# Gate projections ahead of split branch projections, and expert rows picked by a 0/1 matrix, in a hybrid encoder step

## The reference

```python
z = x @ w_in                       # q, k, v | xr | gr | gl: 768 + 1024 + 1024 + 2048 columns
attn = sink_attention(rope(q), rope(k), v)          # 8 heads, chunks of 64, a window of two chunks and the meta keys
rnn = scan(a, u)(conv(xr)) * gelu(gr)               # RG-LRU, gates from two block-diagonal products
g = sigmoid(gl + b_gate)                            # 1024 for attention, 1024 for the recurrence
mix = (g_attn * (attn @ w_branch_attn) + g_rnn * (rnn @ w_branch_rnn)) @ w_out
x = layer_norm(ALPHA * x + mix)
# hierarchical experts: best group of 4, best two of its 4 experts
for e in range(16):
    h = silu(x @ w_gate[e]) * (x @ w_up[e])         # 1024 -> 512
    y = y + combine[:, e:e+1] * (h @ w_down[e])     # 512 -> 1024
x = layer_norm(ALPHA * x + y)
```

## Time and profile before

| | us |
|---|---|
| median of 3 runs (636.44 to 639.0) | 638.3 |
| the profiled execution | 637.03 |
| its span | 635.2 |
| TensorE matmuls busy (84% of the span) | 536.4 |
| VectorE busy | 230.0 |
| ScalarE busy | 133.5 |
| GpSimd busy | 68.5 |

### The profile page before, as it was taken

How to read it: one execution, slowest core, us unless ns; L and a number is a source line. 1 busy time by engine, 2 the same in 40 slices (tenths; PEclk the granted TensorE clock), 3 DMA queues, 4 the chain that set the end, 5 groups by cost and what they waited for, 6 DMA issues and landing times.

```text
span 635.2 us, 9071 instructions
## 1 busy us (share of the span) xinstructions
PE 536.4 (84%) x3552; PEld 393.7 (62%) x3553; DVE 230.0 (36%) x488; ACT 133.5 (21%) x245; POOL 68.5 (11%) x87
## 2 busy tenths in 40 slices
PE   4789989999999999999973699899787898687840
PEld 1789956887889798878663465555443455354410
DVE  2925985777332223113346021211111111111177
ACT  3344287852512122100020000000000000000010
POOL 4160730000000000010000710100000000000210
PEclk9999989877999999999975799999879799989895
DMA  8237791402156879790075389999999999999642
GB/s 220 98 97 219 191 297 44 134 1 68 33 194 203 299 247 313 268 358 10 33 308 205 100 318 385 381 387 376 391 397 401 414 412 410 397 423 426 252 124 83
DMA packets 55213, 157.49 MB, mean 248 GB/s; under 512 B 3558, under 2 KB 36034, under 8 KB 51076
## 3 DMA queue, kind: packets, MB, share of 16 engines
q1 hardware_dynamic: 46464, 135.11, 57.0%
q0 software_dynamic: 4896, 13.92, 7.6%
q10 hardware_dynamic: 3812, 7.88, 3.5%
HBM read 145.10 MB, written 11.78 MB: 247 GB/s over the span
## 4 chain that ended last, share of the span: by engine, by line
PE 66%; DMA 15%; DVE 7%; issue 4%; ACT 3%; SPq 3%; DVEq 0%; POOL 0%; POOLq 0%; ACTq 0%
PE bank L1031 20%; DMA expert_slots<-in_w_up 10%; PE bank L842 8%; PE bank L992 7%; PE bank L829 6%; PE bank L830 6%; PE bank L831 6%; SPq L590 3%; PE bank L917 3%; PE bank L1024 2%; DMA z_rows<-work 2%; PE bank L811 1%; PE bank L897 1%; PE bank L812 1%; PE bank L813 1%
## 5 line engine op out<-in xcount | busy, mean ns | idle before, releaser
L1031 PE MATMUL bank<-expert_slots,work 128*64 128x256 f32 (+3 forms) x1584 | 190.2, 414 | 30.8 <-DMA expert_slots<-in_w_gate 12.3
L1031 PEld LDWEIGHTS bank<-expert_slots,work 128*64 128x64 f32 (+1 forms) x1584 | 105.3, 138 | 104.3 <-issue 48.9
L829 PE MATMUL bank<-z_high,weights_high 128*128 128x320 f32 (+1 forms) x256 | 81.8, 319 | 0.4 <-DVE weights_low L536 0.4
L830 PE MATMUL bank<-z_low,weights_high 128*128 128x320 f32 (+1 forms) x256 | 80.2, 313 | 0.0
L831 PE MATMUL bank<-z_high,weights_low 128*128 128x320 f32 (+1 forms) x256 | 80.0, 313 | 0.0
L1749 DVE SCALAR_TENSOR_TENSOR work<-work,bank 128x256 f32<-128x256 f32 (+1 forms) x18 | 7.3, 406 | 142.4 <-ACT work L1316 136.5
L842 PE MATMUL bank<-work,expert_slots 128*128 128x320 f32 x192 | 52.3, 432 | 0.0
L536 DVE TENSOR_TENSOR weights_low<-expert_slots,weights_high 128x2048 fp32r<-128x2048 f32 x19 | 43.5, 2288 | 22.8 <-ACT weights_high L531 22.7
L829 PEld LDWEIGHTS bank<-z_high,weights_high 128*128 128x128 f32 x256 | 49.1, 192 | 1.6 <-DVE weights_low L536 0.7
L830 PEld LDWEIGHTS bank<-z_low,weights_high 128*128 128x128 f32 x256 | 48.9, 191 | 0.2
L831 PEld LDWEIGHTS bank<-z_high,weights_low 128*128 128x128 f32 x256 | 48.7, 190 | 0.0
(11 more groups left out here) (252 smaller groups left out, 566.1 us busy)
## 6 DMA issues: line engine op xcount, KB each, us to landing
expert_slots<-in_w_gate SPq DMA_DIRECT2D x16, 2048.0 KB, 28.9
expert_slots<-in_w_up SPq DMA_DIRECT2D x16, 2048.0 KB, 31.6
expert_slots<-in_w_down SPq DMA_DIRECT2D x15, 2048.0 KB, 28.7
expert_slots<-in_w_in SPq DMA_DIRECT2D x19, 1024.0 KB, 5.8
expert_slots<-in_w_branch_rnn SPq DMA_DIRECT2D x4, 1024.0 KB, 7.2
expert_slots<-in_w_out SPq DMA_DIRECT2D x4, 1024.0 KB, 5.8
expert_rows<-work ACTq DMA_DIRECT2D x30, 128.0 KB, 8.4
expert_rows<-work POOLq DMA_DIRECT2D x6, 384.0 KB, 10.6
```

The source lines that it names most:

```text
L829: nc.tensor.matmul(b[:, 0:NALL - lo], wh[:, k, o], zh[:, k, lo:NALL], start=(k == 0), stop=False)
L830: nc.tensor.matmul(b[:, 0:NALL - lo], wh[:, k, o], zl[k // 4][:, k % 4, lo:NALL], start=False, stop=False)
L1031: mm = nc.tensor.matmul(bank[m * j:m * j + m, cols], lhsT(k), rhs(k, j), start=(k == 0), stop=(k == kk - 1))
```

## The change

Six things are changed. (1) The order of the input projections: all sixteen gate channels follow the gr channels, as fillers of attention and then alone, and the branch projections come after them. Four fillers stand in chunk 0 and two in each later chunk. (2) Weights are rounded and subtracted in half units of 128 columns, four ahead of TensorE. (3) The branch projections use the three split products too; attention and recurrent results are split for it, the latter into the place of the tokens' high part. The recurrence gates' tanh stays in the place of expert 1's down weights, so SyncE waits for the last merge before it loads those. (4) Scores are issued so that the two head groups alternate, and the V products take 256 columns at once with the groups alternating. (5) The ranks come from three products over prefix sums. VectorE makes from them, for each item, a 0/1 matrix of tokens by places; TensorE multiplies it with the token rows in SBUF, for 64 rows per item (two halves of the channels on the two column halves), ScalarE copies, TensorE transposes and VectorE copies as before. The rest pass picks its 32 rows itself. Indirect gathers remain for overflow items only. (6) The product that lists tokens is made after item 0, and the residual's scaling moves from GpSimd to ScalarE at the end.

The diff, cut to its core:

```diff
-SPLIT = [*range(U_MERGE)] + [u for u in range(U_MERGE, U_OUT) if (u - U_MERGE) % 4 < 2]
-SPLIT_AT = ((9, 0), (10, 1), (11, 3))
+AHEAD = 4
+P_XR, P_GR, P_GATE, P_PROJ, P_END = (2 * u for u in (U_XR, U_GR, U_GATE, U_PROJ, U_OUT))
+GATES = [(kind, m) for kind in ("ga", "gl") for m in range(KD)]
+PROJS = [(kind, m) for p in range(0, KD, 2) for kind in ("pa", "pr") for m in (p, p + 1)]
+FILLERS = [("gr", c) for c in range(KD)] + GATES
+FILL = [4, 2, 2, 2, 2, 2]
+FILLED = [sum(FILL[:c]) for c in range(len(FILL) + 1)]
...
+        gl_tanh = slots[:, 2 * EXP - KF * D:2 * EXP - KF * D + KD * NTOK].rearrange("p (k n) -> p k n", n=NTOK)
+        rnn_h = z_high[:, 0:KD * NTOK].rearrange("p (k n) -> p k n", n=NTOK)
+        rnn_l = rnn_low[:, :].rearrange("p (k n) -> p k n", n=NTOK)
+        attn_h = attn_high[:, :].rearrange("p (k n) -> p k n", n=NTOK)
+        attn_l = attn_low[:, :].rearrange("p (k n) -> p k n", n=NTOK)
...
+        def piece_of(n):
+            u = n // 2
+            kk = KD // 2 if u >= U_PROJ and (u - U_PROJ) % 2 == 0 else KD
+            return u, slice(0, kk), slice(P * (n % 2), P * (n % 2) + P)
+        def high_of(eng, n):
+            u, ks, cols = piece_of(n)
             unit_loaded(eng, u)
-            if n >= 2:
-                unit_consumed(eng, SPLIT[n - 2])
-            nc.scalar.copy(high[n % 2], ring[u % RING]).then_inc(high_made, 1)
...
+        def low_of(eng, n):
+            u, ks, cols = piece_of(n)
+            eng.wait_ge(high_made, n + 1)
+            nc.vector.tensor_tensor(low[u % RING][:, ks, cols], raw[u % RING][:, ks, cols], high[n % AHEAD][:, ks, :], ALU.subtract)\
                 .then_inc(low_made, 1)
...
                     expert_part(*divmod(part, 3))
                 if u == U_OUT + 1:
+                    sp.wait_ge(merge_made, KD)
                     expert_part(1, 2)
             for u in range(U_OUT, NUNIT):
...
+                    out=xg[0:CAP, :], out_offset=None, in_=z1_dram[:, :],
+                    in_offset=bass.IndirectOffsetOnAxis(ap=index_i[0:CAP, i:i + 1], axis=0)).then_inc(xg_in, 16)
             pool.wait_ge(route_done, 1)
             pool.wait_ge(z1_out, 48)
-            for i in range(NE):
-                if i >= 3:
-                    pool.wait_ge(xt_full, i - 2)
-                gather(i, i % 3)
-                if i == 2:
-                    scale_residual()
             pool.wait_ge(ctrl_done, 1)
...
+            def chan_split(n, rhs):
+                pe.wait_ge(low_made, n + 1)
+                wh, wl = parts(n)
+                b = M.claim(pe, chan_of(n))
+                kk = piece_of(n)[1].stop
                 for k in range(kk):
-                    mm = nc.tensor.matmul(b[:, 0:n], w[:, k, o:o + P], rhs(k), start=(k == 0), stop=(k == kk - 1))
-                mm.then_inc(M.f_full(name), 1)
+                    xh, xl = rhs(k)
+                    o = b[:, 0:xh.shape[-1]]
+                    nc.tensor.matmul(o, wh[:, k, :], xh, start=(k == 0), stop=False)
+                    nc.tensor.matmul(o, wh[:, k, :], xl, start=False, stop=False)
+                    mm = nc.tensor.matmul(o, wl[:, k, :], xh, start=False, stop=(k == kk - 1))
+                mm.then_inc(M.f_full(chan_of(n)), 1)
...
             def scores(c):
-                for g in range(4):
-                    kv, half = divmod(g, 2)
-                    hp = slice(HD * kv, HD * kv + HD)
-                    b = S.claim(pe, ("S", c, g))
-                    q = qT[hp, c, P * half:P * half + P]
+                for half in range(2):
+                    pair = (half, 2 + half)
+                    into = [S.claim(pe, ("S", c, g)) for g in pair]
+                    rows_of = [slice(HD * kv, HD * kv + HD) for kv in range(NKV)]
...
+                for i, (at, n) in enumerate(blocks):
+                    for kv in range(NKV):
+                        if c == 4:
+                            v = (vW if i == 0 else vS)[0:n, HD * kv:HD * kv + HD]
+                        elif i == len(blocks) - 1:
+                            v = vM[0:n, HD * kv:HD * kv + HD]
+                        else:
+                            v = qkv[0:n, i, QKV - P + HD * kv:QKV - P + HD * kv + HD]
+                        mm = nc.tensor.matmul(b[HD * kv:HD * kv + HD, 0:2 * P], v, pT[0:n, i, 2 * P * kv:2 * P * kv + 2 * P],
+                                              start=(i == 0), stop=(i == len(blocks) - 1))
                 mm.then_inc(M.f_full(("PV", c)), 1)
...
                 M.emptied(pe, name)
-            gr = iter(range(KD))
+            def fill(lo, hi):
+                for f in range(lo, hi):
+                    chan_split(P_GR + f, tokens(META))
             for c in range(CHUNKS + 1):
...
-                if p == 0:
-                    M.emptied(pe, ("PV", CHUNKS - 1))
-                for m in (p, p + 1):
-                    chan(u + 2, m, ("pa", m), lambda k: attnT[:, k, :], 4)
-                if p == 0:
-                    pe.wait_ge(rnn_made, 2)
-                for m in (p, p + 1):
-                    chan(u + 3, m, ("pr", m), lambda k: rnnT[:, k, :], KD)
+            fill(FILLED[-1], len(FILLERS))
+            for q, (kind, m) in enumerate(PROJS):
+                if q == 0:
+                    pe.wait_ge(attn_low_made, 1)
+                if q == 2:
+                    pe.wait_ge(rnn_low_made, 2)
+                if kind == "pa":
+                    chan_split(P_PROJ + q, lambda k: (attn_h[:, k, :], attn_l[:, k, :]))
+                else:
+                    chan_split(P_PROJ + q, lambda k: (rnn_h[:, k, :], rnn_l[:, k, :]))
...
-            for k in range(2):
+            flat = "p j e -> p (j e)"
+            nc.tensor.matmul(b[:, 0:NE], before, e_sum[:, 0, :], start=True, stop=True)
+            nc.tensor.matmul(b[:, NE:4 * NE], ones, e_upto.rearrange(flat), start=True, stop=False)
+            nc.tensor.matmul(b[:, NE:3 * NE], before, e_sum[:, 1:3, :].rearrange(flat), start=False, stop=True)\
+                .then_inc(S.f_full("ranks"), 1)
...
+            def picked(bank, cols, s, at, n):
+                parts = P // n
                 for j in range(3):
-                    mm = nc.tensor.matmul(b[0:CAP, 0:NITEM], rank_hot[:, k, CAP * j:CAP * j + CAP], item_hot[:, k, NITEM * j:NITEM * j + NITEM],
-                                          start=(k == 0 and j == 0), stop=(k == 1 and j == 2))
-            mm.then_inc(S.f_full("index"), 1)
-            pe.wait_ge(route_done, 1)
-            def turn(i, s, n):
-                pe.wait_ge(xg_in[s], 16 * (n + 1))
+                    m = OUT_ROWS[j]
+                    z = rows[0:m, j, :].rearrange("t (p k) -> t p k", k=KD)
+                    for q in range(parts):
+                        mm = nc.tensor.matmul(bank[n * q:n * q + n, cols], pick[s][0:m, j, at:at + n],
+                                              z[:, :, KD // parts * q:KD // parts * (q + 1)], start=(j == 0), stop=(j == 2))
+                return mm
+            def choose(i, s):
+                pe.wait_ge(pick_made, i + 1)
+                picked(TB[0], slice(0, 512), s, 0, FIRST).then_inc(pick_full, 1)
+            def turn_chosen(i):
+                pe.wait_ge(pick_taken, i + 1)
                 wait_past(pe, xt_made, i)
-                cols = xg[s][0:CAP, :].rearrange("c (p k) -> c k p", k=KD)
+                four = rows_of.rearrange("c (p k) -> c k p", k=4)
+                for k in range(4):
+                    mm = nc.tensor.transpose(TB[1][:, P * k:P * k + P], four[:, k, :], ident)
+                mm.then_inc(xt_full, 1)
...
+                    choose(i + 1, (s + 1) % 3)
                     hidden(i, s, n, ha_full)
+                    if first and s == 1:
+                        pe.wait_ge(route_done, 1)
                     if not (first and s == 0):
                         down(i - 1, (s - 1) % 3, n if s else n - 1)
-                    turn(i + 1, (s + 1) % 3, n + (s + 1) // 3)
+                    turn_chosen(i + 1)
+                    if first and s == 0:
+                        pe.wait_ge(ctrl_done, 1)
                     maybe_rest(i, s, n)
                     turn_hidden(ha_made, i + 1, hta_full)
-            turn(0, 0, 0)
+                    if first and s == 0:
+                        overflow_index()
+            choose(0, 0)
+            turn_chosen(0)
...
-            for p in range(0, KD, 2):
-                for w, name in enumerate(("ga", "gr_gate")):
-                    for m in (p, p + 1):
-                        if m >= 2:
-                            act.wait_ge(merge_made, m - 1)
-                        b = M.arrived(act, (name, m))
-                        run(mtmp[m % 2][w], b[:, 0:NTOK], ACT.Tanh, bias=hbg[:, KD * w + m:KD * w + m + 1], scale=0.5)\
-                            .then_inc(M.f_free((name, m)), 1)
-                if p < KD - 2:
-                    high_of(act, SPLIT[13 + p])
-                    high_of(act, SPLIT[14 + p])
+            M.emptied(act, ("PV", CHUNKS - 1))
```

(74 more changed lines are left out.)

400 lines of the change are left out of this document (198 added, 202 removed).

## The result

The changed kernel takes 687.3 us (median of 4, 686.0 to 692.3) against 638.7 in the same session: ratio 1.082, 95% interval 1.076 to 1.087. The forecast was 617, with 602 to 633 for eight times in ten. The profiled execution has a span of 686.4 us, 51.2 more than before; its granted clock is 0.913.

What follows compares the result with a forecast made beforehand. TensorE was taken to bound the kernel up to 324 us, routing to 356, expert-weight loads from 366. The terms summed to -20.2 us against the profiled 637.0, so 616.8, predicted 617, with 602 to 633 for eight times in ten.

Steps and rivals of the forecast that it cites:

- Expert loop: Items 3 to 14: DMA engines are relieved, but TensorE pays for choosing, 14.3 us an item; +4.1 us (-4 to +10).
- the third: Rival for the expert items: choosing not paired or its moving operand slow, 36 us more, 653 us; chance 0.12.
- choosing above 3.5 us an item: Sign in the expert loop that the prediction was wrong; choosing was forecast at 2.8 us an item.
- Output weights: Output projection: late loads behind expert 1's 2 MB down weights, a 3.6 us stall plus 0.8 for clock; +4.4 us (0 to 8).
- Rounding ahead of the gates: Before ScalarE's recurrence activations: one half-unit rounding of about 1 us remains of two whole-unit ones; -2.2 us (-3.5 to 0).
- Branch projections: Input side: 96 k-steps as split products at 0.438 us instead of plain at 0.538; -9.6 us.
- attention: Attention chunks: wider, alternating PV products, paired scores and half the slow clock's loss regained; -12 us (bounds -5 and -18).
- new waits: Before the merge: rounding the recurrent result takes 5.0 us, two attention projections cover 3.5; +1.5 us (0 to 3).
- unit loads: In the merge: a recurrent unit lands about 10.6 us after issue, 2.4 late once; +2.5 us (0 to 6).
- Routing: From the ranks to the first weight refill: gathers leave the path, 21.0 us instead of 29.9; -8.9 us (-12 to -4).

Runs made afterwards that it cites:

- the short rest: The changed kernel with the rest pass's gate and up products issued together, 32 matmuls fewer per item in TensorE's loop: 632.4 us, 0.992 of before.
- the padded kernel before: The kernel before with 4, 8 or 18 never-run matmuls behind each rest (405, 417, 447 in the body): 638.7, 683.2, 679.1 us.
- loads and rounding put right: The changed kernel with the rest's gate and up products issued together, weight loads reordered and unit 8 rounded later on ScalarE: 612.1 us, 0.959 of before.

## Why the prediction was wrong

The forecast change was -20.2 us and the measured one +51.2. By its steps:

**Expert loop, +4.1: failed, +60.0.** The step counted what each added instruction costs when it runs, and got that right: items at 14.32 us against 14.3, and 230.2 us for the stretch in the version with the short rest, against 230.1. What failed is that code was taken as free of cost but for its run time. The change's rest pass (14 more matmuls an item) is in the stream of every item though it runs in two of the sixteen. That makes 42 of the 48 matmuls by which the body grew, and the choosing, less the transposes it saves, the other 6; together they took it past what TensorE keeps, which in the padded kernel before lies between 405 and 417. This is 55.8 us, some two thirds idle time and a third the clock that falls in it. None of the rivals had it; the third, the slow choosing, named the right sign and the wrong cause, and "choosing above 3.5 us an item" is seen only behind a stall. The clue was there before the prediction: the trace of the kernel before has a queue named instruction, and its packets all but stop after the loop's first round.

**Output weights, +4.4 (0 to 8): +9.2.** The order was read rightly: one stall, at the weights behind the 2 MB. It was mis-sized, 6.9 us of wait instead of 3.6, and 2.3 for the rest instead of 0.8. The forecast had the unit land 10.7 us after SyncE was released, behind one part of 2 MB; the chain has 13.6 from its issue. Why it took 13.6 is not shown.

**Rounding ahead of the gates, -2.2 (-3.5 to 0): +5.5, outside its bounds.** The step looked at what ScalarE rounds after the last copy and missed that rounding four half units ahead also needs those units that much earlier. Unit 8, issued at 75.6 us with GpSimd's writes of zeros in flight, landed at 88.6 us; ScalarE stood idle 8.9 us for it, with the copy of xr channel 7 queued behind.

**Branch projections, attention, new waits, unit loads, together -17.6: -16.5.** The split products run at the rate forecast (0.146 us). Attention was better than its 12, by difference 14.8 (16.5 less 9.6, plus the 7.9 of waits below). The clock row, which answers to the earlier trace rows, is full, where the forecast gave back only half of the 8.4 us that the slow clock cost. And the V products, 48 records of 256 columns in place of 96 of 128, take 6.7 us over the five chunks against 8.6 forecast:

```profile
120.00:160.00 40.00, 40.00 (x309) 35.89 (x308) 35.38 (x83) 28.39 (x63) 0.00 (x0) 1.00 0.34 110
```

The merge gave some of that back: 2.5 us for the low part of the recurrent branch and 5.4 in two waits for rounded weights, against 1.5 and 2.5. The recurrent units landed 10.9 us after issue (median), as the forecast had it (10.6), but TensorE waited twice and not once. That attention's miss and the merge's nearly cancel is luck.

**Routing, -8.9: -7.3.** 22.6 us from the ranks to the refill against 21.0. Up to the end of the hidden product the forecast is met: 18.5 us, against 18.6 without the prefix sums, which run ahead of the ranks. From there to the refill it took 4.0 in place of 2.0, and the reason is the one of the loop: behind the skipped rest of item 0 TensorE waits 2.7 us for nothing that the profile shows.

```profile
358.00 0.44 PE L1093 MATMUL bank<-const,work 128*128 128x128 f32 x2 [2.72 <-issue]
```

With the short rest this wait is gone and the stretch takes 20.6 us (335.7 to 356.2). Another 1.2 us were lost ahead of the ranks, some 0.3 of it the prefix sums; the rest is open.

**The sum.** Without the fetching of code the change comes to 632.4, 0.8% below before, not 617. Stretch by stretch, the short-rest version's profiled execution lies 14 us above the forecast: the start of the gates 6.8 (unit 8), the output weights 5.0, the merge 1.4, the stretch ahead of the ranks 1.2, the routing -0.4, the loop 0.1. With loads and rounding put right it is at 612, inside the range.

## What to carry to other kernels

The code in a loop's body has a size, and branches that are seldom taken count in full. Before adding to a long hardware loop, look at whether the instruction queue falls silent after its first round. If it does, ask how much room there is (matmuls that never run, added until the queue no longer falls silent, measure it), and make the rare branch short rather than fast. If TensorE waits for "issue" at a wrap or behind a branch while packets of instructions keep coming, suspect this first. When work is prepared further ahead, ask of each engine that does it in order what it must wait for, and what stands behind it.

## What was not expected of the hardware

TensorE kept a body of 405 matmuls (all but 33 of them fp32 products, each two weight loads and two products in the trace) and not one of 417, and at the bound the whole kernel went from 638.7 to 683.2 us. A wrap that has to fetch costs 6.3 to 6.5 us of the chain in the changed kernel. Behind two of its three wraps the granted clock is 0.50 for the twelve products (5.58 us against 2.87), behind the third 0.59 (4.84 us). With the loop written out and the DMA engines 0.92 busy (455 to 600 us), code in sequence waited 0.8 us once, but a skipped branch up to 3.7 us; in the bodies that are fetched again code in sequence waited too, up to 4.1 us. Not every skipped branch costs: those of items 2 and 3 in the changed kernel cost nothing. That the code counted, and not the work done, is shown by the versions with never-run code; how the chip picks what to keep was not tested.
